# Seven-product down projection of a two-layer decoder: weight differences from VectorE to GpSimd, and 29 such turns instead of 24

## What is computed

```python
def swiglu(h, w_gate, w_up, w_down):
    return (jax.nn.silu(h @ w_gate) * (h @ w_up)) @ w_down   # h 256x1024, w_gate/w_up 1024x2816, w_down 2816x1024

x += 1/2 * swiglu(rms(x))    # four times: before and after each layer's mixer and cross-attention
```

## Time and profile before

| | |
|---|---|
| device time, three runs | 1177.59, 1177.66, 1177.66 us (median 1177.66) |
| span of the profiled execution | 1175.6 us; its own device time is not listed apart from the three runs, which lie 2.0 to 2.1 us above the span |
| busy share | TensorE 99%, VectorE 81%, ScalarE 62%, GpSimd 11% |
| granted TensorE clock | 0.999 |
| mean DMA rate | 196 GB/s |

### The profile page before, as it was taken

How to read it: one execution, slowest core, us unless ns; L and a number is a source line. 1 busy time by engine, 2 the same in 40 slices (tenths; PEclk the granted TensorE clock), 3 DMA queues, 4 the chain that set the end, 5 groups by cost and what they waited for, 6 DMA issues and landing times.

```text
span 1175.6 us, 17562 instructions
## 1 busy us (share of the span) xinstructions
PE 1169.0 (99%) x6769; PEld 1022.7 (87%) x6769; DVE 957.0 (81%) x1144; ACT 727.7 (62%) x967; POOL 131.0 (11%) x127
## 2 busy tenths in 40 slices
PE   9999999999999999999999999999999999999998
PEld 8888889889989888888888888889887898888886
DVE  6687898875657589889988979997886676797998
ACT  7566555854457566667565757564576566675773
POOL 1010001420142010100010001010012121100000
PEclk9999999999999999999999999999999999999999
DMA  9966755454445455979765779947623434678891
GB/s 322 332 207 199 200 194 179 145 179 144 144 143 180 144 181 173 270 218 268 226 202 166 229 217 263 269 145 213 209 89 135 135 118 156 208 225 251 245 258 69
DMA packets 168337, 230.71 MB, mean 196 GB/s; under 512 B 15312, under 2 KB 139600, under 8 KB 168144
## 3 DMA queue, kind: packets, MB, share of 16 engines
q1 hardware_dynamic: 163664, 213.30, 55.9%
q0 software_dynamic: 4464, 16.25, 7.3%
q10 hardware_dynamic: 144, 0.26, 0.1%
HBM read 213.02 MB, written 1.05 MB: 182 GB/s over the span
## 4 chain that ended last, share of the span: by engine, by line
PE 99%; POOL 0%; DVE 0%; issue 0%; POOLq 0%; DVEq 0%
PE ps L2334 30%; PE ps L2341 16%; PE ps L2313 15%; PE ps L2314 15%; PE ps L2315 15%; PE ps L2417 1%; PE ps L2611 1%; PE ps L3075 1%; PE ps L2931 1%; PE ps L3098 0%; PE ps L2619 0%; PE ps L3111 0%; PE ps L3036 0%; PE ps L3033 0%; PE ps L2485 0%; PE ps L2683 0%
## 5 line engine op out<-in xcount | busy, mean ns | idle before, releaser
L2334 PE MATMUL ps<-hT,w_parts 128*128 128x512 f32 x1568 | 374.9, 391 | 0.0
L2334 PEld LDWEIGHTS ps<-hT,w_parts 128*128 128x128 f32 x1568 | 290.0, 188 | 58.2 <-ACT w_parts L807 0.4
L1368 DVE TENSOR_TENSOR w_parts<-raw,w_parts 128x2048 fp32r<-128x2048 f32 x85 | 196.1, 2316 | 57.9 <-ACT w_parts L754 57.9
L2341 PEld LDWEIGHTS ps<-hT,w_parts 128*128 128x128 f32 x1568 | 201.4, 191 | 8.0 <-DVE w_parts L1444 0.2
L754 ACT ACTIVATE w_parts<-raw 128x2048 fp32r<-128x2048 f32 x85 | 162.3, 1920 | 72.8 <-PE ps L2315 69.8
L889 ACT ACTIVATE w_parts<-raw 128x2048 fp32r<-128x2048 f32 x108 | 206.0, 1907 | 0.6 <-DMA raw<-in_ffn_w_gate 0.6
L2341 PE MATMUL ps<-hT,w_parts 128*128 128x256 f32 x1568 | 204.1, 283 | 0.0
L1616 DVE TENSOR_TENSOR w_parts<-raw,w_parts 128x2048 fp32r<-128x2048 f32 x63 | 143.9, 2284 | 1.2 <-ACT w_parts L889 1.2
L2313 PE MATMUL ps<-w_parts,arena_r 128*128 128x512 f32 (+1 forms) x234 | 91.2, 390 | 0.0
L2314 PE MATMUL ps<-w_parts,arena_r 128*128 128x512 f32 (+1 forms) x234 | 91.1, 389 | 0.0
L2313 PE MATMUL ps<-w_parts,hT 128*128 128x512 f32 (+1 forms) x240 | 91.0, 379 | 0.0
(11 more groups left out here) (375 smaller groups left out, 2123.5 us busy)
## 6 DMA issues: line engine op xcount, KB each, us to landing
raw<-in_ffn_w_down SPq DMA_DIRECT2D x44, 1024.0 KB, 5.0
raw<-in_ffn_w_gate SPq DMA_DIRECT2D x43, 1024.0 KB, 5.4
raw<-in_ffn_w_up SPq DMA_DIRECT2D x43, 1024.0 KB, 5.4
raw<-in_xattn_wkv SPq DMA_DIRECT2D x16, 1024.0 KB, 5.3
xn<-arena POOLq DMA_DIRECT2D x30, 512.0 KB, 5.6
raw<-in_even_w_in SPq DMA_DIRECT2D x13, 1024.0 KB, 5.1
raw<-in_xattn_wq SPq DMA_DIRECT2D x8, 1024.0 KB, 5.1
raw<-in_xattn_wo SPq DMA_DIRECT2D x8, 1024.0 KB, 5.3
```

The source lines that it names most:

```text
L1368: ins = V.tensor_tensor(lo, src, hi.bitcast(F32), ALU.subtract)
L2334: mm(ps[:, bank0 + m, :], cols(w_hi, n, k, CW, m * P, (m + 1) * P), hT[:, k, :, :].rearrange("p a c -> p (a c)"), start=k == 0, stop=False)
L2341: last = mm(ps[:, bank0 + m, SEQ:], cols(w_lo, n, k, CW, m * P, (m + 1) * P), hT[:, k, 0, :], start=False, stop=k == KT - 1)
```

## The change

Mixed turns are now 4 to 8 in stage 0 (five) and 1 to 8 in stages 1 to 3 (eight each): 29. The four subtractions of the down chunk's blocks are GpSimd's, which waits for the raw chunk. The first difference has a tile of its own, `w_first` (in `xk`, 512 columns), so no block of `raw` is overwritten. The split of the down chunk falls into two: columns 512 to 2047 are split straight from `raw` (VectorE then raises `down_split`, on which SP's next down load waits), and the first 512 columns of the parts hold `w_first`, split after `w_sums`. One VectorE order (`turn_mixed`) serves all mixed turns. `mixed_down` takes block numbers and banks in another order, still 21 matmuls. GpSimd's list for stage 0 stands ahead of `norm(1)`; in stages 1 to 3 it stands behind the norm as before. `kept` is in `xn` in all stages; the semaphores are shared between the stages.

```diff
@@ class Mixed
-            FIRST, COUNT = (2, 0, 0, 0), (3, 7, 7, 7)
+            TURN, COUNT = (4, 1, 1, 1), (5, 8, 8, 8)
             w_sums = part(3072, [3, 512])
+            w_first = xk[:, 6:8, :].rearrange("p a c -> p (a c)")
...
-            kept = [copied, kept_later, kept_later, kept_later]
+            kept = kept_later
@@ sync, turn of ffn
-                        if not (first and isinstance(j, int) and j == 0 and c == 0):
+                        if c == 2 and after_mixed:
+                            behind = Mixed.TURN[f] + 1
+                            sp.wait_ge(down_split, j + (down_split_at(f, 0) + 1 - behind))
+                        elif not (first and isinstance(j, int) and j == 0 and c == 0):
                             sp.wait_ge(lo_done, j * 3 + (n - RING + 1))
@@ scalar, turn of ffn
                     if out is not None:
+                        act.wait_ge(mixed_mm, out + (mixed_mm_at(f, 0) + 1))
+                        copied(0)
                     act.wait_ge(chunks_used, j * 3 + (base + 2))
...
                     if out is not None:
+                        copied(1)
-                    if mixed is not None and (f or out is not None):
-                        sums_hi()
-                    split(base + 4 + RING)
+                    if mixed is None:
+                        split(base + 4 + RING)
+                    else:
+                        m = (base + 4) % RING
+                        act.wait_ge(raw_in[m], (j - 1) * 16 + landed(base + 4 + RING))
+                        nc.scalar.activation(w_hi[:, m, 512:], raw[:, m, 512:], ACT.Copy).then_inc(hi_done, 1)
+                        act.wait_ge(w_summed, mixed * 4 + (w_sums_at(f, 0) + 4))
+                        nc.scalar.activation(Mixed.w_hi, Mixed.w_sums, ACT.Copy)
+                        nc.scalar.activation(w_hi[:, m, 0:512], Mixed.w_first, ACT.Copy).then_inc(w_sums_hi, 1)
@@ vector, turn_mixed (the order of turn_mixed_next, changed)
                     gate_sum(j)
                     gate_scale(j)
                     split(base + 2 + RING)
...
                     gu_sum(i, 2, Mixed.gu_sums[:, 1, :], gu_blocks[:, 1, :], gu_blocks[:, 0, :], ALU.subtract)
-                    dve.wait_ge(raw_in[m % RING], (j - 1) * 16 + landed(m))
-                    dve.wait_ge(lo_done, j * 3 + (base + 2))
-                    w_sum(i, 0, Mixed.w_sums[:, 0, :], slot[:, 3, :], slot[:, 1, :])
                     gu_sum(i, 3, Mixed.gu_sums[:, 2, :], gu_blocks[:, 2, :], Mixed.gu_sums[:, 1, :], ALU.subtract)
-                    w_sum(i, 1, slot[:, 1, :], slot[:, 1, :], slot[:, 0, :])
-                    w_sum(i, 2, Mixed.w_sums[:, 1, :], slot[:, 3, :], slot[:, 1, :])
-                    dve.wait_ge(gu_hi_done, j + (f * FJ + 1))
-                    V.tensor_tensor(Mixed.gu_lo, Mixed.gu_sums, Mixed.gu_hi.bitcast(F32), ALU.subtract)
-                    w_sum(i, 3, Mixed.w_sums[:, 2, :], slot[:, 2, :], Mixed.w_sums[:, 1, :])
-                    hidden_lo(j, gu_hi, gu_lo)
                     split(base + 3 + RING)
-                    dve.wait_ge(w_sums_hi[f], w_sums_hi_at(f, i) + 1)
+                    hidden_lo(j, gu_hi, gu_lo, mixed=True)
+                    n, m = base + 4 + RING, (base + 4) % RING
+                    dve.wait_ge(hi_done, (j - 1) * 3 + (n + 1))
+                    dve.wait_ge(w_summed, i * 4 + (w_sums_at(f, 0) + 4))
+                    V.tensor_tensor(w_lo[:, m, 512:], raw[:, m, 512:], w_hi[:, m, 512:].bitcast(F32),
+                                    ALU.subtract).then_inc(down_split, 1)
+                    dve.wait_ge(w_sums_hi, i + (w_sums_hi_at(f, 0) + 1))
                     V.tensor_tensor(Mixed.w_lo, Mixed.w_sums, Mixed.w_hi.bitcast(F32), ALU.subtract)
-                    split(m)
+                    V.tensor_tensor(w_lo[:, m, 0:512], Mixed.w_first, w_hi[:, m, 0:512].bitcast(F32),
+                                    ALU.subtract).then_inc(lo_done, 1)
@@ vector, turns of a stage
+                first = Mixed.TURN[f]
+                turn_mixed(first, 0)
+                with dve.Fori(1, Mixed.COUNT[f]) as i:
+                    turn_mixed(i + first, i)
+                turn_read(FJ - 2, Mixed.COUNT[f] - 1)
@@ gpsimd, ffn
+                def w_sum(i, c, dst, a, b):
+                    if c:
+                        pool.wait_ge(w_summed, w_sums_at(f, i) + c)
+                    G.tensor_tensor(dst, a, b, ALU.subtract).then_inc(w_summed, 1)
+
+                for i in range(Mixed.COUNT[f]):
+                    n = n0 + 3 * (Mixed.TURN[f] + i)
+                    pool.wait_ge(raw_in[n % RING], landed(n))
+                    pool.wait_ge(lo_done, n - RING + 1)
+                    w_sum(i, 0, Mixed.w_first, blocks[:, 0, :], blocks[:, 1, :])
+                    w_sum(i, 1, Mixed.w_sums[:, 1, :], blocks[:, 2, :], Mixed.w_first)
+                    w_sum(i, 2, Mixed.w_sums[:, 0, :], blocks[:, 2, :], blocks[:, 0, :])
+                    w_sum(i, 3, Mixed.w_sums[:, 2, :], blocks[:, 3, :], Mixed.w_sums[:, 1, :])
+                    if i > 1:
+                        for half in range(2):
+                            pool.wait_ge(mixed_read, mixed_read_at(f, i - 1) + half + 1)
+                            if f or i > 2:
+                                pool.wait_ge(kept_added_in[half], kept_added_at(f, i - 1))
+                            pool.dma_start(Mixed.kept[half], Mixed.copied[half],
+                                           accum_op=ALU.add).then_inc(kept_added_in[half], 16)
```

More of the change, by code:

```diff
@@ L504, in build, with mixed_no, down_split_at @@
         es = even_sems
[L506 to L510, removed]
+        w_summed, w_sums_hi, gu_summed = quarters_lo, quarters_hi, up_half_in
+        mixed_mm, mixed_read, down_split = halves_hi, quarter_in[0], quarter_in[1]
         kept_added_in = [sem(f"kept_added_in{half}") for half in range(2)]
+        def mixed_no(f, i):
+            return sum(Mixed.COUNT[:f]) + i
         def kept_added_at(f, i):
[L515 to L523, removed]
+            return (sum(Mixed.COUNT[:f]) - 2 * f + i - 1) * 16
         def w_sums_at(f, i):
[L526 removed]
+            return 4 * mixed_no(f, i) + 4
         def w_sums_hi_at(f, i):
[L529 removed]
+            return mixed_no(f, i) + 3
         def gu_sums_at(f, i):
[L532 removed]
+            return 4 * mixed_no(f, i) + 16
         def mixed_mm_at(f, i):
[L535 removed]
+            return mixed_no(f, i) + 3
         def mixed_read_at(f, i):
[L538 removed]
+            return 2 * mixed_no(f, i) + 8 * f + 16
+        def down_split_at(f, i):
+            return mixed_no(f, i) + 16
         class Odd:
@@ L668, in ffn @@
             def ffn(layer, which, first=False):
-                base = at["ffn", layer, which]
+                f, base = 2 * layer + which, at["ffn", layer, which]
                 gate, up = (d[w][layer, which].rearrange("(k p) (j c) -> j p k c", p=P, c=CW)
@@ L714, in ffn @@
                                 sp.dma_start(dst, src).then_inc(small_in, 16)
-                with sp.Fori(8 if first else 0, FJ - 1) as j:
-                    turn(j)
+                    turn(8, True)
+                    turn(9, True)
+                else:
+                    turn(0)
+                    turn(1)
+                    with sp.Fori(2, FJ - 1) as j:
+                        turn(j, True)
                 n = base + FFN_CHUNKS - 1
@@ L955, in ffn @@
                     turn(4, lambda c: c and squares(1, mem_rows, lambda t, h: act.wait_ge(mem_in, 16), tiles=(c - 1,)),
[L956 to L961, removed]
+                         mixed=0)
                 else:
                     turn(1, mixed=0)
[L964 to L970, removed]
+                first = Mixed.TURN[f]
+                turn(first + 1, mixed=1, out=0)
+                turn(first + 2, mixed=2, out=1, added=True)
+                with act.Fori(3, Mixed.COUNT[f]) as i:
+                    turn(i + first, mixed=i, out=i - 1, added=True)
+                if f == 0:
+                    turn(FJ - 2, small_tables)
+                else:
+                    turn(FJ - 2)
                 made[0] = base + FFN_CHUNKS - 1
@@ L2262, in ffn @@
             def ffn(f):
-                for i in range(1, Mixed.COUNT[f] - 1):
-                    for half in range(2):
-                        pool.wait_ge(mixed_read[f], mixed_read_at(f, i) + half + 1)
-                        if f > 1 or i > 1:
-                            pool.wait_ge(kept_added_in[half], kept_added_at(f, i))
-                        pool.dma_start(Mixed.kept[f][half], Mixed.copied[half],
-                                       accum_op=ALU.add).then_inc(kept_added_in[half], 16)
+                n0 = at["ffn", f // 2, f % 2] + 4
+                blocks = raw[:, n0 % RING, :].rearrange("p (a c) -> p a c", c=512)
+                def w_sum(i, c, dst, a, b):
[17 more added lines that the diff above has]
```

(6 more changed lines are left out.)

143 lines of the change are left out of this document (40 added, 103 removed).

## The result

The changed kernel takes 1231.61 us (median of 4 runs, 1231.08 to 1232.35), the one before 1177.66. The ratio is 1.0458, 95% interval 1.0444 to 1.0473. That is slower, as forecast, but by 54 us where 8.4 were forecast, and far above the range's end of 1203. The profiled execution has a span of 1230.5 us.

A forecast was written before the change was run, and what follows sets the result against it. It took TensorE, busy 99%, as the bound: 8.1 us of holes in stages 1 to 3, 0.6 in stage 0 and 3.1 at stage ends, less 3.41 saved, gave +8.4 and 1186.0 us; 8-in-10 range 1174 to 1203.

The forecast's parts named there:

- The bound, and the 3.41 us: TensorE, busy 99%, bounds the kernel; five more mixed turns, each with 3 matmuls less, take 3.41 us off.
- The price of one subtraction: A GpSimd subtraction shuts VectorE out for about 1.02 us unless beside a PSUM-input operation or idle time.
- The turn of 16.57: VectorE's mixed turn: 13.43 us of its own plus 3.14 of GpSimd blocking, an excess of 0.7 over TensorE's 15.89.
- ScalarE's 62%: ScalarE's extra instruction and copies were costed at nothing, since its 62% busy share leaves room in each turn.
- Rival (b): All four GpSimd subtractions uncovered in each mixed turn, an excess of 1.5 us a turn: +28, 1206 us; chance 0.12.
- They are done several us before the next chunk lands: GpSimd's two DMA issues a turn, behind its subtractions and waiting for ScalarE's copies, were costed at nothing.
- rival (c): GpSimd's chain becomes the loop, each subtraction waiting behind a full split: 20.5 us a turn, +130 us; chance 0.03.
- Stage 0, `norm(1)`, the order of blocks: `norm(1)` behind `ffn(0)` on GpSimd is wanted only after stage 0; the other block and bank order costs nothing.
- `product` and `gu_sum` lengthened by a subtraction each: Sign on VectorE: `product`, a `gu_sum` or the up split about 1 us longer, three or four times a turn.
- One operation of GpSimd above 2 us: Sign on GpSimd: its four operations spread over 5 us or more, one above 2 us where a split runs.
- VectorE without idle time: Sign in the mixed turns: VectorE has no idle time and its turn is at 16.6 us.
- Holes from the fourth mixed turn on: Sign on TensorE: holes of about 0.7 us ahead of the down product from the fourth or fifth mixed turn.

The follow-up runs named there:

- experiment 2: Changed kernel with GpSimd's four subtractions replaced by short memsets that read nothing, differences left out: 1174.48 us, ratio 0.9975 to the kernel before.
- experiment 3: Changed kernel with GpSimd's four subtractions replaced by memsets, three of them three times as wide, so GpSimd is busy about 5 us without reading: 1174.75 us.
- experiment 8: Changed kernel with two of the four subtractions on GpSimd (those reading only `raw`) and two back on VectorE: 1197.46 us, ratio 1.0171 to the kernel before.
- experiment 9: Changed kernel with two subtractions on GpSimd, two on VectorE, and accumulating DMAs cut to 8 of 512 columns: 1184.37 us, ratio 1.0059 to the kernel before.
- experiment 1: Changed kernel, all four subtractions on GpSimd, with each accumulating DMA cut to 8 of 512 columns: 1205.29 us.

## Why the prediction was wrong

**The bound, and the 3.41 us.** Right. Experiments 2 and 3 show that the 15 matmuls are worth 3.0 when nothing else is paid.

**The price of one subtraction.** Right. The 1.02 us from rows 4 and 5 came back: `product` +0.23 as worked out, the four `gu_sum` +3.05 for three subtractions where 3 x 0.97 was forecast. Experiments 8 and 9 show it for one and two: the four `gu_sum` take 2.25 and 3.22 instead of 1.27.

**The turn of 16.57.** Too low; it is 17.3 where the load lands in time (experiment 1, and the first regime). Of the 0.7 missing, about 0.1 is in VectorE's own part, 0.14 in the blocking, and 0.49 are two waits that were costed at nothing with ScalarE's 62%: 0.36 ahead of L1599 and 0.13 ahead of L1602. The late `gu_sum` release ScalarE's high part (L916), and from there ScalarE has L916, L886, L907 and L925 in a row, 0.43, 0.52, 0.91 and 1.48 us (1094.61 to 1097.95), and VectorE waits for the last. A share of 62% says nothing about a chain that starts late. No run changes ScalarE's order, so this part is read from the trace alone. With an excess of 1.4 instead of 0.7 the forecast's own sum becomes 3 x (7 x 1.4 - 2.2) + (4 x 1.4 - 2.2) + 3.1 - 3.4 = +25.9; experiment 1 is at +27.8. So the sum comes within 2 us once this term is right. Its single parts are not shown by that: in experiment 1 a turn of TensorE is 1.35 us too long, of which at most 0.4 is a hole ahead of the down product, and the rest lies in shorter gaps between its other matmuls. Rival (b) had 1.5 for that term and would have been near, for a reason (all four uncovered) that isn't the one here.

**The step that failed:** of GpSimd's DMA issues, "They are done several us before the next chunk lands", costed at nothing, with the load at its 5.0. Of the 45.6 us between the forecast and the result this step is 26.3 (experiment 1); the other 19.3 are the turn above. The turn alone (1205.3) would have missed the range too. They are done in time, that is true, but the step looked only at what waits behind them on GpSimd and not at what they carry. Before, GpSimd was idle and they went out when ScalarE's copies were ready, the second of them 7 us ahead of the next down load:

```profile
1050.53 0.89 POOL L2269 DMA_DIRECT2D xn<-arena  x1 [47.59 <-ACT arena L908]
1053.95 0.86 POOL L2269 DMA_DIRECT2D xn<-arena  x1 [2.53 <-ACT arena L918]
...
1060.78 0.37 SPq L690 DMA_DIRECT2D raw<-in_ffn_w_down  x1
```

Now they stand behind the subtractions, and the last of these also releases the split on which the down load waits. The two transfers are tied together, and the load takes 8.7. That closes a loop of load, subtractions and split of 18.75 that TensorE isn't part of. It is rival (c), which had 0.03. "Against it: only two full splits lie in that stretch" was right, one of four subtractions waits behind one; the loop closes through the load, which (c) left at 5.2: by its own form, 8.95 with the issue + 8.03 + 1.77 = 18.75.

**Stage 0, `norm(1)`, the order of blocks.** In stage 0 the loss at the last `gate_sum` is 6.3 us against before, then each of the other stages, with the way to it, adds 16.0 to 16.4 (22.7, 38.8, 54.8 at the last `gate_sum` of stages 1 to 3). The losses are alike in the three stages and follow the turns, which leaves no sign of a cost of `norm(1)` or of the block order.

**Signs named beforehand.** `gate_sum` in TensorE's chain, `product` and `gu_sum` lengthened by a subtraction each: seen. One operation of GpSimd above 2 us: seen, 3.38. VectorE without idle time: right in the first regime, wrong in the second, where 2.55 us a turn end with GpSimd's last subtraction. Holes from the fourth mixed turn on: seen in stage 3 (0.35 at 1102.89), but then 1.92, 2.19, 1.02, 2.22 and 1.02 instead of 0.7.

## What to carry to other kernels

Work taken off a full VectorE and given to GpSimd is no relief if both read SBUF: a subtraction of 0.6 us on VectorE shut it out for 1.0 us from GpSimd, and only an operation with a PSUM input or idle time of VectorE covered that. When an engine that only issued DMAs gets work of its own, follow each DMA to its new time and ask which load it now meets, and whether one event releases both. Then close every loop through a buffer (load, first reader, last reader, next load) with the durations as they will be, since it may bound the turn without the busiest engine.

## What the hardware showed that was not expected

- A 1 MB load beside 1 MB of accumulating DMAs took 8.7 us, and 5.0 and 4.8 beside the small ones (experiments 1 and 9). The Trainium skill, page "DMA: Bandwidth & Descriptors", section "Issuing engines are not separate DMA queues", says that DMAs of all engines run on the same 16 DMA engines and interleave. The trace agrees: where the down load and the accumulating DMAs meet (from 1100.00 on), the mean share of the 16 engines reaches 1.01. It isn't proof by itself, since the kernel before reaches 1.02 too (1050 to 1060, where its accumulating DMAs meet an up load). Stretch, length, busy us of PE, PEld, DVE, ACT and POOL, granted clock, DMA share, GB/s:

```profile
1100.00:1110.00 10.00, 9.65 (x49) 7.66 (x48) 9.64 (x12) 7.37 (x9) 1.52 (x2) 1.00 1.01 308
...
1140.00:1150.00 10.00, 9.90 (x37) 8.03 (x38) 9.64 (x12) 7.00 (x8) 4.19 (x2) 0.83 0.89 266
```

- The same table has a granted clock of 0.83 from 1140 to 1150. That is a mean of the clock's two levels, not a level of its own:

```profile
1140.00:1141.00 1.00, 0.90 (x2) 0.81 (x3) 0.96 (x3) 0.20 (x1) 0.00 (x0) 0.50 0.91 221
...
1144.00:1145.00 1.00, 1.00 (x6) 0.80 (x5) 0.93 (x3) 0.64 (x1) 0.00 (x0) 1.00 1.00 404
```

  TensorE had stood for 2.19 us until 1140.10. From 1140 to 1143 the granted clock is at the lower level (0.50, 1.2 GHz), with matmuls 0.43 us apart instead of 0.23, and from 1144 at the upper one. In stage 3 the holes ahead of the down product alternate from there, 2.19, 1.02, 2.22 and 1.02 us, while the turn stays at 18.75: what the lower clock costs comes out of the next hole, and it costs nothing there. Over the span the mean was 0.987, before the change 0.999. Whether the clock lengthened the stage ends is open.
- A chain that shifts by fractions of a microsecond changed who covers whom: 13 us hung on whether one subtraction fell beside `up_sum` or on the `gu_sum` behind it (experiments 8 and 9).
